# Projecting q, k and v by half groups, with attention heads between the row tiles, in a one-core hybrid decoder layer

## The chip, the core and the metric

The program runs on one core of a Trainium2 chip, as one launch. The metric is device time in microseconds (us) of that launch. TensorE is the matrix engine (PE in the profile, PEld its weight loads), VectorE is DVE, ScalarE is ACT, GpSimd is POOL, and SP only issues transfers. All arithmetic inputs are float32.

## The reference, cut to what matters

One layer of a decoder with two mixers on the same normalised input `hn`. The attention mixer has three groups of eight heads; group g has a window and a dilation of (128, 1), (512, 4) or (2048, 16). The prompt has 512 tokens, the decoding batch 8 tokens.

```python
u = hn @ w_in                                  # 520 rows x 1024, q, k, v among its columns
q = _rope(_rmsnorm(q.reshape(b, t, 24, 64), q_norm_w), pos)
k = _rope(_rmsnorm(k.reshape(b, t, 24, 64), k_norm_w), pos)
for g, (win, dil) in enumerate(((128, 1), (512, 4), (2048, 16))):
    o, lse = _dilated_attn_prompt(q[:, :, 8*g:8*g+8], k[...], v[...], win, dil)
    new_bufs.append(stack([kg, vg])[:, -min(win, 512):])
alpha = softmax(stack(lses))                   # groups merged per head slot
```

With 512 prompt tokens, group 0 is attention inside blocks of 128 tokens and to the block before. In groups 1 and 2 a query sees keys of its own residue class modulo 4 (group 2: modulo 16, by a mask). The other mixer is a chunked state-space scan (SSD) with 32 heads. The new key and value rows are outputs too.

## The kernel before

Every weight matrix is cut into items of 1 MB (`ITEMS`), which pass through two slots: SP loads `w_raw`, ACT rounds it to `wH` (float32r), and DVE takes the rest, `wL = w_raw - wH` (the plan's step `split`, L1178 and L1511). A projection adds three products, xH·wH, xL·wH and xH·wL, for each of the eight 128-row pieces of the contraction.

All engines walk one list of steps, `PLAN`, in its order; each engine does its own part of each step and waits on semaphores where it must. So a late step on an engine delays every later step of that engine. PSUM has eight banks. A bank is taken by TensorE (`take`) once whoever read its last content has freed it (`free`).

The attention part treats one group after the other.

- **Rows.** `("rm", g, s, half)` is half of the contraction for the 512 columns of q, k or v of a group. `proj_rows` (L578 to L596) works on five row tiles: four of 128 prompt tokens and one with the 8 decoding tokens. Tokens are the stationary operand and the 512 weight columns the moving one. Five banks, 0 to 4, stay open over the two halves. In groups 1 and 2 the stationary operand takes every fourth token (`slice(B + t, R, NT)`), so that a row tile is a residue class.
- **Norm and rotary, per row tile of q and k.** ACT squares the bank (L1204), DVE sums per head (L1526), ACT takes Ln and Exp (L1210, L1213), DVE multiplies (L1539, frees the bank) and forms the cosine part (L1543), POOL the sine part (L1080), and DVE adds them into `st` (L1552). v is copied by ACT to `vv` (L1191).
- **`turn`.** TensorE transposes `st` into banks 5 to 7, and ACT copies them to `qT` and `kT` (L1286). All four tiles of q are turned in one step, and so are those of k.
- **Heads.** Then come the eight heads: `scores` on TensorE (L678; L685 for the block before, in group 0 only), the scaled and masked copy and the maximum on DVE (L1655 to L1669), the exponentials on ACT (L1294, L1298), `probs`: transposes on TensorE (L694, L699) and copies to `PT` by ACT (and by DVE for the second bank, L1679), `values`: the product with v (L715, L718), copied by ACT to `oU` (L1320) for each pair of heads. ACT's exponentials are part of the step `scores`.
- **Filling.** `BESIDE_HEADS` puts pieces of one row tile (24 matmuls of 512 columns) between the heads of group 0, two between those of group 1, and 96 matmuls of 260 columns of the gate `za` between those of group 2.

After the third group there is a barrier, then the merge of the groups and the decoding tokens' attention, then the SSD part. There `ssdE` (L852 to L856) spreads a row of log decays over 128 partitions for each of a unit's two heads, with a contraction over 64 partitions (`id2`, `ac2`); it does so 16 times.

Of the kernel before, what the change touches and what calls it, by code (L numbers as in the profile page):

```python
# [19 lines left out]
F32 = mybir.dt.float32  # L20
F32R = mybir.dt.float32r
# [33 lines left out]
NKEYS = P  # L55

# [5 lines left out]
def weight_items():  # L62

    items = [("rm", g, s, half) for g in range(NG) for s in "qkv" for half in range(2)]
    items += [("za", 0), ("za", 1), ("dt", 0)]
    for g in range(GROUPS):
        items.append(("bc", g))
        for j in range(2 * g, 2 * g + 2):
            items += [("x", j), ("z", j)]
    items += [("gs", j) for j in range(4)]  # L70
    for j in range(2):
        items += [("ga", 2 * j), ("ga", 2 * j + 1), ("ba", j)]
    items += [("bs", j) for j in range(KD)]
    items += [("wo", j) for j in range(4)]
    return items
# [6 lines left out]
BESIDE_HEADS = {1: {0: 7}, 2: {0: 7, 1: 5}}  # L82
SPREAD_FIRST = 5
SLOTS_S = 5
PHASE_ENDS = (5, 10, 13)

SHAPES = {"rm": (4, 512), "dt": (KD, P), "bs": (UNITS, P), "ba": (4, 512)}


def item_units(i):  # L90

    return tuple(range({"rm": 0, "dt": 1, "bs": 1, "ba": 4}.get(ITEMS[i][0], 2)))


def plan():
# [18 lines left out]
    for g in range(NG):  # L114
        for s in "qkv":
            whole("rm", g, s, 0)
            if (g, s) == (0, "q"):
                out.append(("rope",))
            if s == "v":
                out.append(("turn", g, 0))  # L120
            whole("rm", g, s, 1)
        out.append(("turn", g, 1))


        if g + 1 < NG:
            out.append(("split", ITEM_AT["rm", g + 1, "q", 1]))
            beside = [("rowtile", g + 1, t, k) for t in BESIDE_HEADS[g + 1] for k in range(KD)]
        else:
            beside = []
            for unit in range(2):  # L130
                za_uses.append(proj("za", 0, unit=unit))
                _, i, units = out.pop()
                beside += [("proj", i, units, k) for k in range(KD)]
        total, steps = len(beside), 3 * SLOTS + 2
        count = 0
        for h in range(SLOTS + 2):
            for step in (("scores", g, h), ("probs", g, h - 1), ("values", g, h - 2)):
                if 0 <= step[2] < SLOTS:
                    out.append(step)
                    count += 1  # L140
                    while beside and total - len(beside) < total * (count + 2) / steps:
                        out.append(beside.pop(0))


# [18 lines left out]
    for i in range(n):  # L163
        out.append(("key", i))
        if i == 3:
            out.append(("exps",))
# [85 lines left out]


PLAN = plan()


# [62 lines left out]
def hybrid_kernel(nc, xT, wpack, params, consts, sel_in, state_conv, ssm_in, caches,  # L319
                  y_out, tail_out, ssmp_out, kvp_out, ssms_out, kvs_out):  # L320
    ctx = ExitStack()
    with ctx:
# [3 lines left out]
        def sb(name, shape, dt=F32):  # L326
# [28 lines left out]
        st = a1.tile("st", [P, 2, NT, T])  # L355
        qT = a1.tile("qT", [P, HP, T])
        kT = a1.tile("kT", [P, HP, T])
        vv = a1.tile("vv", [P, NT, T])
        ropeA = a1.tile("ropeA", [P, 2, RT, HD])
        ropeB = a1.tile("ropeB", [P, 2, RT, HD])  # L360
        pt_at = a1.at
        sq = a1.tile("sq", [P, 2, T])
        ss = a1.tile("ss", [P, 2, SLOTS])
        rst = a1.tile("rst", [P, 2, SLOTS])
        qn = a1.tile("qn", [P, T])
        t1 = a1.tile("t1", [P, T])
        t2 = a1.tile("t2", [P, T])
        Sx = a1.tile("Sx", [P, 2, 2 * NT - 1, P])

        PT = Arena(nc, pt_at, end).tile("PT", [P, 2, 2 * NT - 1, P])  # L370
# [70 lines left out]
        ac2 = a3.tile("ac2", [2 * HEADS, T], F32R)  # L441
        id2 = a3.tile("id2", [2 * HEADS, HEADS], F32R)
# [41 lines left out]
        names = """squares_added ac_parts_ready act_order b_rows_ready b_spread_ready b_spread_used bc_samples_kept cache_shifted cached_v_used  # L484
# [4 lines left out]
            gate_ready half_item_used head_pair_out head_scales_ready head_sums_ready  # L489
            k_stored keys_scored keys_turned last_state_ready log_decays_masked masked_cb_ready maxima_sums_ready  # L490
# [4 lines left out]
            sample_dt_ready sample_exponents sample_exps sample_probs sample_probs_turned  # L495
# [3 lines left out]
            states_before_ready tables_loaded v_rows_ready v_stored weight_high_ready  # L499
# [4 lines left out]
        names += [f"cache_loaded{i}" for i in range(RING)]  # L504
# [14 lines left out]
        def cm_bank(i, s, hf):  # L519
            if ITEMS[i] == ("za", 0):  # L520

                return banks[((2, 3), (5, 7))[s][hf]]
# [6 lines left out]
        def qk_count(g, si, t):  # L529
            return (g * 2 + si) * (NT + 1) + t  # L530
# [12 lines left out]
        def pv_done(eng, n):  # L543

            if n % 2:
                g, hp = n // SLOTS, n % SLOTS // 2
                banks[6].full(eng, ("O", g, hp))
# [3 lines left out]
        def row_bank(g, s, t):  # L551

            return banks[BESIDE_HEADS.get(g, {}).get(t, t) if s == "q" else t]

# [4 lines left out]
        merge_banks = [banks[i] for i in (2, 6, 0, 3, 7, 1)]  # L559
# [4 lines left out]
        def _(pe):  # L564
            nbar = [0]
            turn_c = [0]
# [7 lines left out]
            def row_columns(g, t):  # L574
                return slice(0, P) if t == NT else (slice(B + P * t, B + P * (t + 1)) if g == 0 else slice(B + t, R, NT))

            def proj_rows(i, g, s, half):
                for t in range(NT + 1):  # L578
                    if s == "q" and t in BESIDE_HEADS.get(g, {}):
                        continue  # L580
                    bk = row_bank(g, s, t)
                    if half == 0:
                        bk.take(pe, ("rm", g, s, t))
                    cols = row_columns(g, t)
                    for k in range(4):
                        kk = 4 * half + k
                        if t == 0 and (g, s) == (0, "q"):
                            pe.wait_ge(S["x_low_ready"], kk + 1)
                        for n, (a, b) in enumerate(((xH, wH), (xL, wH), (xH, wL))):
                            mm = pe.matmul(bk.tile[:, :], a[:, kk, cols], wslot(b, i)[:, k, :],  # L590
                                           start=(kk == 0 and n == 0), stop=(kk == KD - 1 and n == 2))
                    if half == 1:
                        mm.then_inc(bk.filled, 1)
                    elif t == NT:
                        mm.then_inc(S["half_item_used"], 1)
                ends[i] = (banks[NT].filled, banks[NT].uses["rm", g, s, NT]) if half else (S["half_item_used"], i // 2 + 1)  # L596
# [28 lines left out]
            for step in PLAN:  # L625
# [11 lines left out]
                elif op == "proj":  # L637
# [3 lines left out]
                    if it[0] == "rm":  # L641
                        proj_rows(i, *it[1:])
                    else:
                        proj_cols(i, a[1], a[2] if len(a) > 2 else None, *it)
                elif op == "rowtile":

                    g, t, kk = a
                    i = ITEM_AT["rm", g, "q", kk // 4]
                    pe.wait_ge(S["weight_low_ready"], i + 1)
                    bk = row_bank(g, "q", t)  # L650
                    if kk == 0:
                        bk.take(pe, ("rm", g, "q", t))
# [1391 lines left out]
```

## Time and profile before

| | |
|---|---|
| median of three runs | 1187.37 us (1184.84 to 1188.95) |
| the profiled execution | 1187.57 us |
| its span in the trace | 1185.8 us |
| TensorE busy | 1097.8 us (93%) |
| VectorE, ScalarE, GpSimd busy | 656.7, 499.4, 219.8 us |
| mean granted clock | 0.94 |

A view's time runs from the start of the span. Busy time of PE counts a matmul from its start to its modelled end, and neighbours overlap; the distance from start to start is what tells the rate. "clock" is the granted TensorE clock: 1.00 is 2.4 GHz, 0.50 is 1.2 GHz, and a stretch between has both. Matmuls of full float32 (scores, values) are recorded as two each. The rows themselves are given below in numbered groups.

### The profile page before, as it was taken

What the parts mean: (1) busy time and instruction counts of PE and PEld (TensorE: products, weight loads), DVE (VectorE), ACT (ScalarE), POOL (GpSimd) and SP (SyncE); (2) the same over time, 40 slices, a digit from 0 to 9 for tenths busy, and PEclk for the clock granted to TensorE, in tenths of its full rate; (3) what the DMA queues carried; (4) which work ended last, traced back from release to release, by engine and by line L of the source; (5) the groups of instructions that cost most, each with busy time, mean ns of one, the idle gap of its engine ahead of it and who ended that gap; (6) DMA issues with size and microseconds to landing.
All of it is one profiled execution on the core that took longest, in us unless ns stands there. A gap on an engine that the chain in (4) does not pass through costs nothing.

```text
span 1185.8 us, 19650 instructions
## 1 busy us (share of the span) xinstructions
PE 1097.8 (93%) x7838; PEld 1010.2 (85%) x7838; DVE 656.7 (55%) x936; ACT 499.4 (42%) x1130; POOL 219.8 (19%) x209
## 2 busy tenths in 40 slices
PE   4999989999999989895999999999998999689998
PEld 3887779977988779775999899898998999689998
DVE  6663527622462347237677677776764466834342
ACT  5334533345333544102554645656445566612210
POOL 0330003400231000000211220221120589500000
PEclk9998899989999899756999999999999999789999
DMA  8546102580242047145056246254446899432221
GB/s 348 213 169 276 55 1 116 213 329 1 107 168 81 1 151 246 58 152 232 1 219 235 109 162 254 110 218 163 182 175 273 343 360 343 155 144 80 100 98 46
DMA packets 29819, 198.14 MB, mean 167 GB/s; under 512 B 4104, under 2 KB 6280, under 8 KB 20224
## 3 DMA queue, kind: packets, MB, share of 16 engines
q1 hardware_dynamic: 25712, 183.35, 40.5%
q0 software_dynamic: 4016, 13.54, 3.0%
q8 instruction: 62, 1.02, 0.3%
q14 instruction: 29, 0.24, 0.1%
HBM read 180.16 MB, written 104.70 MB: 240 GB/s over the span
## 4 chain that ended last, share of the span: by engine, by line
PE 73%; DVE 11%; ACT 7%; issue 4%; DMA 2%; POOL 2%; SPq 0%; DVEq 0%; ACTq 0%; POOLq 0%
PE bank L618 36%; PE bank L590 16%; DVE cacc L1575 2%; PE bank L813 2%; PE bank L715 2%; ACT wH L1136 2%; PE bank L678 2%; PE bank L767 2%; POOL t L1080 2%; PE bank L884 1%; PE bank L654 1%; DVE wL L1511 1%; DMA slot<-in_state_ssm 1%; PE bank L902 1%; PE bank L876 1%
## 5 line engine op out<-in xcount | busy, mean ns | idle before, releaser
L1511 DVE TENSOR_TENSOR wL<-w_raw,wH 128x2048 fp32r<-128x2048 f32 (+1 forms) x63 | 145.0, 2302 | 155.0 <-ACT wH L1136 152.9
L618 PE MATMUL bank<-xH,wH 128*128 128x260 f32 x976 | 207.9, 294 | 8.1 <-DVEq L1455 6.9
L618 PE MATMUL bank<-xH,wL 128*128 128x260 f32 x976 | 198.1, 285 | 0.0
L618 PE MATMUL bank<-xL,wH 128*128 128x260 f32 x976 | 197.8, 284 | 0.0
L1136 ACT CAST wH<-w_raw 128x2048 fp32r<-128x2048 f32 (+1 forms) x63 | 119.2, 1892 | 136.2 <-PE bank L618 84.8
L618 PEld LDWEIGHTS bank<-xH,wH 128*128 128x128 f32 x976 | 152.0, 191 | 18.8 <-issue 16.6
L618 PEld LDWEIGHTS bank<-xH,wL 128*128 128x128 f32 x976 | 152.0, 190 | 0.0
L618 PEld LDWEIGHTS bank<-xL,wH 128*128 128x128 f32 x976 | 152.0, 190 | 0.0
L590 PE MATMUL bank<-wH,xH 128*128 128x512 f32 x336 | 136.7, 407 | 10.0 <-DVE xL L1490 6.0
L590 PE MATMUL bank<-wH,xL 128*128 128x512 f32 x336 | 134.6, 401 | 0.0
L590 PE MATMUL bank<-wL,xH 128*128 128x512 f32 x336 | 134.6, 401 | 0.0
L590 PEld LDWEIGHTS bank<-wH,xH 128*128 128x128 f32 x336 | 84.0, 250 | 21.2 <-issue 7.0
L1080 POOL TENSOR_TENSOR t<-qn,ropeB 128x256 f32<-128x256 f32 (+1 forms) x60 | 56.0, 951 | 246.4 <-DVE qn L1539 246.3
L590 PEld LDWEIGHTS bank<-wL,xH 128*128 128x128 f32 x336 | 84.1, 250 | 7.8
L590 PEld LDWEIGHTS bank<-wH,xL 128*128 128x128 f32 x336 | 84.3, 251 | 7.4
L1575 DVE SCALAR_TENSOR_TENSOR cacc<-buf,wcv,cacc 128x544 f32<-128x544 f32 x72 | 56.5, 784 | 17.3 <-ACT cacc L1251 15.1
L1294 ACT ACTIVATE Sx<-Sx,nm 128x128 f32<-128x128 f32 x96 | 37.6, 392 | 57.9 <-DVE nm L1669 57.8
L1381 ACT ACTIVATE Lb<-bank,nac 128x128 f32<-128x128 f32 x128 | 36.7, 369 | 47.1 <-PE bank L862 44.3
L1104 POOL TENSOR_TENSOR Eb<-Eb,CT 128x512 f32<-128x512 f32 x32 | 54.0, 1707 | 11.7 <-ACT Eb L1372 11.7
L618 PE MATMUL bank<-yH,wH 128*128 128x260 f32 x256 | 52.6, 287 | 3.5 <-DVE yL L1928 3.5
L618 PE MATMUL bank<-yL,wH 128*128 128x260 f32 x256 | 52.5, 287 | 0.0
L618 PE MATMUL bank<-yH,wL 128*128 128x260 f32 x256 | 52.2, 285 | 0.0
(285 smaller groups left out, 1916.9 us busy)
## 6 DMA issues: line engine op xcount, KB each, us to landing
w_raw<-in_weights SPq DMA_DIRECT2D x62, 1024.0 KB, 5.3
out_kvs<-in_cache SPq DMA_DIRECT2D x16, 2044.0 KB, 10.2
ring<-in_cache SPq DMA_DIRECT2D x48, 256.0 KB, 3.2
slot<-in_state_ssm SPq DMA_DIRECT2D x16, 512.0 KB, 5.9
out_ssm_s<-slot POOLq DMA_DIRECT2D x16, 512.0 KB, 6.0
out_kvs<-in_cache SPq DMA_DIRECT2D x8, 508.0 KB, 8.8
out_kvp<-st POOLq DMA_DIRECT2D x9, 256.0 KB, 2.3
out_kvp<-vv POOLq DMA_DIRECT2D x9, 256.0 KB, 4.6
```

Of the source, the lines that this page charges most:

```text
L590: mm = pe.matmul(bk.tile[:, :], a[:, kk, cols], wslot(b, i)[:, k, :], start=(kk == 0 and n == 0), stop=(kk == KD - 1 and n == 2))
L618: mm = pe.matmul(bk[hf].tile[:, 0:HALF], wslot(w, i)[:, k, s * P:(s + 1) * P], x[:, k, hf * HALF:(hf + 1) * HALF], start=(k == 0 and n == ...
L678: mm = pe.matmul(bk.tile[:, t * P:(t + 1) * P], qT[o:o + HD, hp, t * P:(t + 1) * P], kT[o:o + HD, hp, t * P:(t + 1) * P], start=True, stop ...
L715: mm = pe.matmul(out, vv[:, t, h * HD:(h + 1) * HD], PT[:, n % 2, t, :], start=(t == 0), stop=True, skip_group_check=True)
L767: mm = pe.matmul(banks[6].tile[:, c:c + B + 1:B], KT[:, n % 2, hp, :], qd[:, q0, :], start=True, stop=True, skip_group_check=True)
L1080: ins = nc.gpsimd.tensor_tensor(o[:, :, x, :], v[:, :, 1 - x, :], rb, ALU.mult)
L1104: nc.gpsimd.tensor_tensor(Eb[:, u % 2, e, :], Eb[:, u % 2, e, :], CT[:, 0:T], ALU.mult).then_inc(S["scaled_c_ready"], 1)
L1136: return nc.scalar.copy(out, in_)
L1294: ins = A(Sx[:, n % 2, t, :], Sx[:, n % 2, t, :], ACT.Exp, bias=nm[:, n % 2, t:t + 1], accum_out=lst[:, g, t, h:h + 1])
L1381: ins = A(Lb[:, e, c, :], banks[5 + e].tile[:, c * P:(c + 1) * P], ACT.Exp, bias=nac[:, c, n:n + 1])
L1511: TT(wL[:, i % 2, 0:k * n], raw[:, i % 2, 0:k * n], wH[:, i % 2, 0:k * n].bitcast(F32), ALU.subtract)\
L1575: ins = STT(out=cacc[:, :], in0=bb[:, w:w + CONV], scalar=wcv[:, cu, w:w + 1], in1=cacc[:, :], op0=ALU.mult, op1=ALU.add)
```

## The change

The unit of work in the attention part becomes a half group `x` (0 to 5), four heads. An item is now all 1024 contraction rows of 256 columns of q, k or v, so there are still 18 such items.

- **Rows.** A row tile of q or k is one step of 24 matmuls with 256 moving columns, in natural token order for all groups. Three banks (0, 1, 2) go round in a ring (`row_ring`) instead of five.
- **v by columns.** The weights are stationary and the tokens move, 260 at a time: 24 matmuls in a slot, two slots for each unit of 128 columns. A unit takes two ring banks; ACT copies them to `vT` (three copies), TensorE transposes `vT` (four transposes and one for the decoding tokens) into a ring bank and bank 6, and DVE copies these to `vv` and `qS`.
- **Residue classes.** For groups 1 and 2 the classes are formed by a strided destination in ACT's copies to `qT`, `kT` and `vT`.
- **Order.** `PLAN` runs over 84 slots (five for q, five for k, four for v of each half group). In slot j: row tile j, exponentials of a head, `roped` of tile j-2, `norm` of j-1, square and sum of j (`copy`), `turn` of j-3, the copies of v, and then a head's scores, probs or values. A head takes four successive slots: scores, exponentials, probs, values. The heads of half group x run beside the row tiles of x+1; those of the last half group beside `za`, in eight slots more.
- **Banks.** All turns, the second probs bank of group 0 and the decoding values share bank 6; scores have bank 3 (and 4), probs bank 5, values bank 7. `qn`, `t1`, `t2` are double, of half width. Stored rows leave in 48 transfers by POOL instead of 24, with half as long rows.
- **SSD.** `ac2` and `id2` get a second copy on partitions 64 to 127, made once by ACT (`dtrows`); the two matmuls of `ssdE` use one half each, and both banks are taken ahead of the first.
- The banks of `za` and of the merge are renamed; step `exps` of the merge becomes `mergeexps`.

```diff
-    items = [("rm", g, s, half) for g in range(NG) for s in "qkv" for half in range(2)]
+    items = [(s, x) for x in range(HALVES) for s in "qkv"]
...
-BESIDE_HEADS = {1: {0: 7}, 2: {0: 7, 1: 5}}
+SLOT_ROWS = 2 * (NT + 1) + 4
...
+    def side_steps():
+        at = {}
+        for n in range(NG * SLOTS):
+            x, m = divmod(n, HH)
+            first, gap = (SLOT_ROWS * (x + 1) + 4 * m, 1) if x < HALVES - 2 else (SLOT_ROWS * (x + 1) + 3 * m, 1)
+            if x == HALVES - 1:
+                first = SLOT_ROWS * HALVES - 2 + 2 * m
+            for d, op in enumerate(("scores", "exps", "probs", "values")):
+                at.setdefault(first + d * gap, []).append((op, n))
+        return at
...
+    def slot(j):
+        mine = at.get(j, [])
+        out.extend(x for x in mine if x[0] == "exps")
+        step("roped", 2)
+        step("norm", 1)
+        step("copy", 0)
+        step("turn", 3)
+        for ago, op in ((0, "vcopy"), (1, "vturn"), (1, "vrows")):
+            if 0 <= j - ago < len(rows) and ITEMS[rows[j - ago][0]][0] == "v" and rows[j - ago][1] % 2:
+                out.append((op, rows[j - ago][0], rows[j - ago][1] // 2))
+        out.extend(x for x in mine if x[0] != "exps")
...
+def row_ring():
+    out, c = {}, 0
+    for step in PLAN:
+        if step[0] == "rows":
+            out["row", step[1], step[2]] = c % 3
+            c += 1
+        elif step[0] == "vcols" and step[3] == 0:
+            for hf in range(2):
+                out["col", step[1], step[2], hf] = (c + hf) % 3
+            c += 2
+        elif step[0] == "vturn":
+            out["vturn", step[1], step[2]] = c % 3
+            c += 1
+    return out
...
+                    for kk in range(KD):
+                        for n, (x, w) in enumerate(((xH, wH), (xL, wH), (xH, wL))):
+                            mm = pe.matmul(bk.tile[:, 0:HC], x[:, kk, row_columns(t)], wslot(w, i)[:, kk, :],
+                                           start=(kk == 0 and n == 0), stop=(kk == KD - 1 and n == 2))
...
+                elif op == "vcopy":
+                    b0, b1 = (col_bank(i, unit, hf) for hf in range(2))
+                        by_class = vT[:, unit, 0:T].rearrange("p (r j) -> p j r", r=NT)
+                        cp(by_class[:, 0:first // NT, :], b0.tile[:, B:HALF].rearrange("p (j r) -> p j r", r=NT))
+                    free(b0)
+                    free(b1)
...
-                        pe.matmul(bk.tile[:, :], id2[:, 2 * u + e:2 * u + e + 1].to_broadcast([2 * HEADS, P]), ac2[:, :],
+                        o = 2 * HEADS * e
+                        pe.matmul(bk.tile[:, :], id2[o:o + 2 * HEADS, 2 * u + e:2 * u + e + 1].to_broadcast([2 * HEADS, P]), ac2[o:o + 2 * HEADS, :],
```

## Rows read from the trace of the kernel before

**Rows 1.** The page, part 2: TensorE busy and granted clock in 40 slices.
```profile
PE   4999989999999989895999999999998999689998
PEclk9998899989999899756999999999999999789999
```

**Rows 2.** Windows: each head stretch and the SSD stretch (stretch, us, busy by engine, clock).
```profile
106.43:167.14 60.71, 52.41 (x322) 44.74 (x320) 29.80 (x65) 33.01 (x129) 0.52 (x1) 0.83 0.16 64
250.01:296.93 46.92, 42.75 (x225) 34.35 (x224) 14.54 (x25) 25.24 (x81) 0.52 (x1) 0.89 0.21 83
378.49:426.50 48.01, 40.73 (x273) 35.15 (x272) 14.53 (x25) 26.28 (x82) 0.52 (x1) 0.89 0.01 2
562.40:913.00 350.60, 345.55 (x2849) 317.62 (x2848) 240.51 (x378) 190.69 (x426) 63.53 (x73) 1.00 0.44 171
```

**Rows 3.** The chain that ended last, whole span: start, us, what.
```profile
18.95 71.80 PE bank L590 x300
90.74 1.88 PE bank L668 x16
92.62 13.98 PE bank L590 x60
571.18 5.76 PE bank L618 x48
```

**Rows 4.** The chain in 140 to 170 us: one head of group 0.
```profile
152.59 0.22 PE bank L718 x2
153.83 1.10 PE bank L678 x8
155.06 0.70 DVE Sx L1655
158.31 0.54 ACT Sx L1294 x3
159.97 1.16 ACT Sx L1298 x6
161.13 0.48 ACT PT L1136
161.79 0.63 PE bank L694 x4
```

**Rows 5.** Groups of instructions by line, whole span: busy us, mean ns.
```profile
L1511 DVE TENSOR_TENSOR wL<-w_raw,wH 128x2048 fp32r<-128x2048 f32 x62 | 143.8, 2320 | 154.7 <-ACT wH L1136 152.6 <-DVE zs L1608 1.7 <-DVE zg L1566 0.2
L1136 ACT CAST wH<-w_raw 128x2048 fp32r<-128x2048 f32 x62 | 118.1, 1905 | 135.9 <-PE bank L618 84.8 <-PE bank L590 43.9 <-DMA w_raw<-in_weights 4.6
L1080 POOL TENSOR_TENSOR t<-qn,ropeB 128x256 f32<-128x256 f32 x48 | 45.1, 960 | 241.9 <-DVE qn L1539 241.9
L1204 ACT ACTIVATE sq<-bank 128x512 f32<-128x512 f32 x24 | 14.3, 599 | 34.2 <-PE bank L590 34.2
```

**Rows 6.** The same view, ScalarE only, 19 to 430 us.
```profile
L1210 ACT ACTIVATE ss<-ss,epsc 128x8 f32<-128x8 f32 x24 | 7.2, 298 | 12.5 <-DVE ss L1526 12.5
```

**Rows 7.** The tile oU: shortest, median, longest copy; group 0 contiguous, others strided.
```profile
L1136 ACT COPY oU<-bank x12: 587/1076/1109, 138.1 to 425.3; 128x512 f32<-128x512 f32 x12
```

**Rows 8.** Timeline of VectorE at the start.
```profile
24.51 1.92 DVE L1490 TENSOR_TENSOR xL<-xw,xH 128x520 fp32r<-128x520 f32 x3
27.12 2.29 DVE L1511 TENSOR_TENSOR wL<-w_raw,wH 128x2048 fp32r<-128x2048 f32 x1 [0.69 <-ACT wH L1136]
32.77 0.46 DVE L1500 SCALAR_TENSOR_TENSOR ropeB<-con,par 128x288 f32<-128x288 f32 x1
```

**Rows 9.** Windows around one gap of TensorE and the clock behind it.
```profile
158.00:162.80 4.80, 2.21 (x13) 1.65 (x12) 1.03 (x5) 4.20 (x17) 0.00 (x0) 1.00 0.00 0
162.80:166.20 3.40, 3.40 (x21) 3.40 (x22) 0.56 (x1) 0.26 (x1) 0.00 (x0) 0.50 0.00 0
```

**Rows 10.** Timeline of TensorE in one SSD unit.
```profile
602.22 1.09 PE L884 MATMUL bank<-Lb,xdt 128*64 128x128 f32 x16
603.24 0.72 PE L855 MATMUL bank<-ac,id 64*128 64x512 f32 x2
```

More of the change, by code:

```diff
@@ L112, in whole @@
         out.append(proj(*item))
[L114 to L142, printed above, removed]
@@ new lines, in plan, with step @@
+    rows = []
+    for i in range(3 * HALVES):
+        rows += [(i, t) for t in (range(4) if ITEMS[i][0] == "v" else range(NT + 1))]
+    za_steps = []
+    def slot(j):
+        def step(op, ago):
+            if 0 <= j - ago < len(rows):
+                i, t = rows[j - ago]
+                if ITEMS[i][0] != "v" and (op != "turn" or t < NT):
+                    out.append((op, i, t))
+        mine = at.get(j, [])
[8 more added lines that the diff above has]
+        out.extend(x for x in mine if x[0] != "exps")
@@ new lines, in plan @@
+    for j, (i, t) in enumerate(rows):
+        if t == 0 and ("split", i + 1) not in out:
+            out.append(("split", i + 1))
+        out.append(("vcols", i, t // 2, t % 2) if ITEMS[i][0] == "v" else ("rows", i, t))
+        if j == 0:
+            out.append(("rope",))
+        slot(j)
+    j = len(rows)
+    for unit in range(2):
+        za_uses.append(proj("za", 0, unit=unit))
+        _, i, units = out.pop()
+        za_steps += [("proj", i, units, k) for k in range(KD)]
+    late = max(at) + 1 - j
@@ L145, in tiles @@
+    for d in range(late):
+        out += za_steps[len(za_steps) * d // late:len(za_steps) * (d + 1) // late]
+        slot(j + d)
     def tiles(item, unit):
@@ L527, in wslot, with qk_count, kept_tiles, k_stores @@
             return w[:, i % 2, 0:k * n].rearrange("p (k n) -> p k n", k=k)
-        def qk_count(g, si, t):
-            return (g * 2 + si) * (NT + 1) + t
+        def qk_count(i, t):
+            return (2 * (i // 3) + i % 3) * (NT + 1) + t
+        def kept_tiles(x):
+            return (NT - 1,) if x < 2 else range(NT)
+        def k_stores(t, x):
+            return 16 * sum(t in kept_tiles(y) for y in range(x + 1))
+        def v_stores(x):
+            return 16 * sum(len(kept_tiles(y)) + 1 for y in range(x % 2, x + 1, 2))
         CV = {}
@@ L545, in pv_done, with row_bank, col_bank, turn_bank @@
             if n % 2:
-                g, hp = n // SLOTS, n % SLOTS // 2
-                banks[6].full(eng, ("O", g, hp))
+                banks[7].full(eng, ("O", n // 2))
             else:
                 eng.wait_ge(S["even_head_summed"], n // 2 + 1)
-        def row_bank(g, s, t):
-            return banks[BESIDE_HEADS.get(g, {}).get(t, t) if s == "q" else t]
+        def row_bank(i, t):
+            return banks[ROW_RING["row", i, t]]
+        def col_bank(i, unit, hf):
+            return banks[ROW_RING["col", i, unit, hf]]
+        def turn_bank(i, unit):
+            return banks[ROW_RING["vturn", i, unit]]
+        def score_bank(n):
+            return banks[3 if n < SLOTS else 3 + n % 2]
         def spread_bank(i):
             return banks[((7, 5) if i < 2 else (7, 6) if i < SPREAD_FIRST else (4, 6))[i % 2]]
-        merge_banks = [banks[i] for i in (2, 6, 0, 3, 7, 1)]
+        merge_banks = [banks[i] for i in (7, 0, 1, 2, 6, 3)]
         block = ctx.enter_context(nc.Block())
@@ L572, in barrier, with row_columns @@
                     pe.wait_ge(S["phase_ended"], 5 * nbar[0])
[L574 to L596, printed above, removed]
+            def row_columns(t):
+                return slice(0, P) if t == NT else slice(B + P * t, B + P * (t + 1))
             def proj_cols(i, units, tile, kind, j):
```

528 lines of the change are left out of this document (290 added, 238 removed).

## The prediction

> **What bounds the kernel now.** I read the page's slices first: TensorE is busy nearly everywhere, but between slices 3 and 15 its clock falls several times [rows 1]. Then the chain, for the true rate. TensorE runs 60 matmuls of 512 columns in 13.98 us, 233 ns each, and 48 of 260 columns in 5.76 us, 120 ns each; 16 transposes take 1.88 us [rows 3]. So a matmul costs what its columns cost (0.45 ns each), and a wide one isn't cheaper by column. Then the windows: the attention part is TensorE work from 18.95 us [rows 3] to 426.50 us [rows 2], 407.5 us, and the three head stretches in it run at a mean clock of 0.83, 0.89 and 0.89 [rows 2].
>
> How much of the 407.5 us is work? Row tiles: 1080 matmuls x 0.233 = 251.6. Turns: 96 transposes x 0.117 = 11.3. A head of group 0 has 7 score and 7 value matmuls, two records each at 0.11 [rows 4], and 7 transposes: 3.9 us, with some 0.1 at each of four changes of kind 4.3. A head of the others has 4 of each, 2.6. That is 8 x 4.3 + 16 x 2.6 = 76. The `za` pieces: 96 x 0.120 plus changes, 13.9. Sum 352.8. So about 55 us are lost now, nearly all in and just ahead of the heads: 17 us in group 0's 60.7, and about 10 in each of the other two, after taking out heads, pieces and turns.
>
> **The change part by part.**
>
> Work. q and k: 60 row tiles x 24 matmuls x 0.1185 (256 columns, by the rate above) = 170.6. v: 24 slots x 24 x 0.120 = 69.1. Turns 11.3 as before. v's transposes are new: 12 x 5 x 0.117 = 7.0. Heads 76, `za` 13.9. Sum 347.9, that is 4.9 less; the gain is v's, which had five row tiles and now has no tile for the eight decoding tokens. Everything else depends on what the new order loses.
>
> Start. The first row tile now needs all eight pieces of x at once. The last arrives at 24.51 + 1.92 = 26.4 us, and DVE is then in wL and the rotary tables until 33.2 [rows 8]. Before, five banks let TensorE go on meanwhile. Now the fourth row tile needs the first bank back: sum, Ln and Exp, multiply, about 1.6 us after 33.2. It starts at 34.9, with 8.5 us of work done since 18.95. Loss 7.4.
>
> Group 0's heads among row tiles (half groups 0 and 1, beside the rows of 1 and 2). Take the slot of a head's scores as j, its start as 0. Row tile 2.85, turn 0.25, scores 1.0, and 0.8 for the block before: TensorE leaves at 4.85. DVE starts when the first score bank is full, at 4.4, and needs 3.25 us to the exponentials (155.06 to 158.31); these take until 161.2, 2.9 us [rows 4]. So ACT is held until 4.4 + 3.25 + 2.9 = 10.6. Only then come, in ACT's order, Ln and Exp of row tile j (0.3 [rows 6] plus 0.2), the next square (0.6 at 512 columns [rows 5], 0.4 here) and the turn's copy. Waiting behind it are DVE's `norm` of j, which frees that row tile's bank at 11.5, and bank 6, free at 12.0. TensorE, meanwhile, has finished slot j+1 at 7.95. Four cases, by where the head falls in the 14 slots:
> - head 1: slot j+2 needs bank 6 twice (turn, then the second probs bank, each emptied before the other). It ends at 14.45 where its work would end at 12.0. Loss 2.5.
> - head 0: v's transpose has used up a ring bank, so the third row tile shares the first's bank, and waits for `norm` of the scores slot. DVE has had wL (2.3 us [rows 5]) and v's rows ahead of the scores. Loss 4.7.
> - head 2: v's first unit takes two ring banks at once, the second being that of tile j, free at 11.5; then wH (1.9 us [rows 5]) stands ahead of the turn's copy. Loss 3.9.
> - head 3: its exponentials stand ahead of `vcopy` (1.1 us), and the next row tile needs a bank that `vcopy` frees. Loss 4.0.
> With 0.3 between v's units this is 15.4 for each of two half groups, and 1.3 twice more where the last head's probs wait for bank 6 behind DVE's copy of v: 33.4.
>
> Groups 1 and 2. DVE takes 1.8 and ACT 1.6 for a head. The same four places lose 2.5, 0, 1.5 and 2.4, and 1.3 between v's units, because the strided copies cost more: a strided copy of 512 columns takes 1.08 against 0.59 [rows 7], so a turn's copy about 0.6 and `vcopy` about 1.5. That is 7.7 in each of two half groups, 6.7 in the last, where heads are three slots apart. The first half group, without heads, loses 2.9 at v's two changes. The tail (four heads beside `za`, DVE and ACT needing 3.7 us where TensorE has 4.5 us of other work) loses 1. A copy that writes 512 bytes apart isn't in the trace; from below it costs as a contiguous one, from above twice the strided one, together -7 to +12 us; I take the strided row.
>
> The sum of losses: 7.4 + 2.9 + 33.4 + 15.4 + 6.7 + 1 = 66.8.
>
> Clock. Now, a stretch of 4.8 us in which TensorE is busy 2.2 is followed by 3.4 us at 0.50, that is at 1.2 GHz [rows 9]. Each such stretch costs at least 1.7 us of work. The new order has six gaps of 3.6 to 4.7 us (heads 0, 2 and 3, twice). Bounds 0 and 12; I take 7.
>
> SSD. The two matmuls of `ssdE` take 0.72 us [rows 10]. The nearest row for small matmuls on different parts of the array is L884, 16 in 1.09 us [rows 10], where records of that size otherwise stand 0.11 apart [rows 4] and would take 1.8: its pairs, into the two column halves, run together. If row halves do so too, a pair saves about 0.3; sixteen pairs, in a stretch where TensorE is busy 345.6 of 350.6 us [rows 2]: -4. Bounds 0 and -5. The Trainium skill, TensorE: Matmul & The Clock Gate, Part 3 (row/col tiling), says that matmuls on distinct row groups run concurrently; by it the -5 holds, and no row here shows it for rows.
>
> At nothing: ACT's one copy of `ac2` (512 columns, some 0.6 us like the square of that width [rows 5]) stands in front of a wait for TensorE's last product of `dtrows`, which comes later than it. POOL's sine pair falls from 2 x 0.96 [rows 5] to some 1.1 in slots of over 3 us; even with five transfers to issue for v it is done before `roped` two slots later. Were that cover gone, about 1 us per v item, 6 in all. The weights' transfers are asked for two items ahead, some 28 us. Doubling the stored transfers costs only POOL's time. The renamed banks move no wait by more than a few tenths.
>
> Sum against the profiled execution, 1187.6 (the median shown is 0.2 lower): work -4.9, losses 66.8 - 54.7 = +12.1, clock +7, SSD -4: +10. I predict **1198 us**.
>
> **The rivals.**
> 1. Interleaving pays. The 33.4 and 15.4 + 6.7 us of ACT's lag are worked out head by head; if the engines catch up better, for instance because DVE gets to the scores sooner, and half of this (28) and the clock's 7 go away, the time is 1163; with all of it gone 1135. For it: ACT and DVE are idle half of every head stretch [rows 2], and heads no longer wait for a whole group's rows and turns. Against it: one head's exponentials block ACT for 2.9 us, and there are three ring banks where there were five. It decides once the losses with the clock fall by 10 us, i.e. below 64. The Trainium skill, Trace Analysis, Optimization Strategy, says that interleaving stretches with different busiest engines may improve performance; by it this rival holds. The same section reads regular gaps as a sign of too little SBUF or PSUM for the next tile, which is my own forecast's mechanism.
> 2. Gains and losses cancel: 1184 to 1191.
> 3. A copy or a bank is worse than I take it: strided writes at twice the strided row, bank 6 shared by turns, probs and v at more places, or clock stretches over 12 us. 1215 to 1230.
> 4. 256-column matmuls are held by their weight loads, and cost more than 118 ns: at 190 ns (the recorded load) q and k would take 103 us more, near 1300. The 260-column row at 120 ns, with a load each, speaks against it.
>
> **How the numbers follow.** 0.48 for my forecast (1191 to 1214), 0.33 for rival 1 (1140 to 1183), 0.10 for rival 2, 0.07 for rival 3, 0.02 for rival 4. What a measurement here can tell from no change is about 0.3%, 3.6 us. Rival 2 and the edges of its neighbours give 0.10 for the same; rival 1 and a little of rival 2 give 0.34 for faster; the rest, 0.56, is slower. The range, 8 in 10, takes in the strided copy's bound, a full clock loss, and half of ACT's lag gone: 1160 to 1214. The forecast's own range is 1191 to 1214.
>
> **What would show it.** In the changed trace the row matmuls should stand 118 to 120 ns apart; TensorE should wait, in the half groups beside group 0's heads, for DVE's `norm` multiply and for ACT (turn copies, `vcopy`), 15 us in each; the PE clock should show half-speed stretches behind these; the attention part should end near 440 us; the `ssdE` pair should start within some 10 ns. I am wrong if the attention part ends before 426 us: then ACT and DVE kept up, and the waits for them are under a microsecond a head. I am also wrong if the row tiles' pitch, or the stretch after the barrier, moves by more than a few us.

## The result, and the profile after

The changed kernel takes 1244.41 us (median of four runs, 1241.26 to 1246.80); the kernel before took 1187.30 us beside it. The ratio is 1.048, 95% interval 1.046 to 1.051. Slower was right, the size was not: 57 us where I had 10, and outside the range.

The profiled execution took 1241.26 us, 53.7 more than the one of before. The page of the changed kernel, parts 1 and 2, against [rows 1]:

```profile
PE 1124.1 (91%) x8834; PEld 1065.1 (86%) x8834; DVE 689.7 (56%) x1082; ACT 527.2 (43%) x1266; POOL 236.4 (19%) x293
...
PE   4979788899999889989599999999999898789998
...
PEclk9989999999999965555699999999999899889999
```

Read the line PEclk first. Its 15th to 20th digits are 6, 5, 5, 5, 5, 6: six slices at about half clock, where before there were three (7, 5, 6). TensorE is hardly idle there: the busy digits above them are 8 and 9, but for a 5 above the last. What is lower early on is its busy time (7 and 8 in the 5th to 8th digit), where heads now stand among the rows.

Windows over the four parts of the span (attention, decoding, the projection of `dt`, SSD and the rest) show what each contributes: stretch, us, busy time of PE, PEld, DVE, ACT and POOL, clock, DMA share, GB/s. After:

```profile
18.95:433.02 414.07, 368.55 (x2868) 347.12 (x2869) 230.16 (x415) 192.03 (x565) 88.11 (x168) 0.98 0.34 132
433.02:592.28 159.26, 142.93 (x1011) 134.19 (x1011) 55.31 (x83) 26.57 (x43) 0.00 (x0) 0.54 0.34 116
592.28:617.49 25.21, 16.34 (x94) 15.91 (x95) 19.04 (x33) 6.21 (x13) 0.00 (x0) 0.64 0.66 255
617.49:1239.50 622.01, 594.25 (x4859) 566.68 (x4858) 375.03 (x537) 290.79 (x630) 148.07 (x121) 0.97 0.47 180
```

The first three parts in the kernel before:

```profile
18.95:426.50 407.55, 383.76 (x1872) 335.34 (x1873) 198.25 (x271) 164.11 (x429) 69.52 (x84) 0.95 0.34 133
426.50:537.57 111.07, 99.32 (x1011) 90.76 (x1011) 55.22 (x83) 26.47 (x43) 0.00 (x0) 0.77 0.50 166
537.57:562.40 24.83, 16.66 (x94) 16.23 (x94) 18.68 (x31) 5.60 (x12) 0.00 (x0) 0.64 0.64 259
```

The attention part is 6.5 us longer, the SSD part 1.4 shorter, the projection of `dt` 0.4 longer. Two changes partly cancel in the attention part: TensorE's idle time grew from 23.8 to 45.5 us, and its time at half clock fell from 44.4 to 13.7 us. The decoding part (merge of the groups, cached keys and values) is 48.2 us longer: the same 1011 matmuls, with VectorE and ScalarE equally busy, at a clock of 0.54 in place of 0.77. Nothing in this part was changed but names of banks.

What happens at its start? TensorE, in the timeline of the changed kernel:

```profile
441.96 0.60 PE L811 MATMUL bank<-con,lst 128*8 128x128 f32 x4
442.40 0.60 PE L829 MATMUL bank<-con,ring 128*128 128x128 f32 x4
448.61 0.77 PE L668 MATMUL bank<-xH,wH 128*128 128x260 f32 x2 [5.61 <-DVEq L1547]
449.18 0.64 PE L668 MATMUL bank<-xL,wH 128*128 128x260 f32 x2
```

The same piece of `za` in the kernel before:

```profile
437.36 0.48 PE L618 MATMUL bank<-xH,wH 128*128 128x260 f32 x2 [0.86 <-DVEq L1455]
```

VectorE, in the timeline of the changed kernel:

```profile
442.15 0.68 DVE L1800 COPY mT<-bank 8x512 f32<-8x512 f32 x1 [0.24 <-DVE qd L1792]
442.97 0.68 DVE L1800 COPY lT<-bank 8x512 f32<-8x512 f32 x1
...
447.36 1.04 DVE L1800 COPY lT<-bank 8x512 f32<-8x512 f32 x1
```

TensorE transposes the six merge tiles into six banks, and DVE copies them out in the order maxima, sums, group by group (L1800). Behind the first cached key's transposes (L829) stands the first piece of `za`'s second unit, which takes banks 2 and 3. In the kernel before these two held the tiles copied first and second. The diff rewrites the list `merge_banks`, from (2, 6, 0, 3, 7, 1) to (7, 0, 1, 2, 6, 3). The first three entries hold the maxima of the groups and the last three the sums, so the copies, which go by turns, took the banks as 2, 3, 6, 7, 0, 1 before, and take them as 7, 2, 0, 6, 1, 3 now: bank 3 is the last of six. The piece waits 5.61 us, until that copy ends at 448.4. Before, the same wait was 0.86 us. The clock's records in the trace show half from 445.5 us, 2.5 us into the wait, for 150.2 us without a break. Behind the wait TensorE is busy all the time by the profile (89.39 of 89.40 us) and still at half:

```profile
448.60:538.00 89.40, 89.39 (x417) 89.40 (x418) 24.50 (x27) 19.61 (x30) 0.00 (x0) 0.50 0.34 119
```

The last cached key ends at 540 us. Before, the keys ran at full clock, and this part had 54.6 us at half, from 487.1 on, behind the last key. So some 95 us at half are new, and they lie in the wait and the keys.

### The profile page after: what moved, and what is told of

The parts are those of the page before. It is cut to its first block, busy times and chain, and to the rows that moved or that the text cites. A ratio compares the mean times of both kernels' runs of the same rounds, so it can differ in the third digit from the quotient of the medians.

```text
span 1239.5 us, 22367 instructions
## 1 busy us (share of the span) xinstructions
PE 1124.1 (91%) x8834; PEld 1065.1 (86%) x8834; DVE 689.7 (56%) x1082; ACT 527.2 (43%) x1266; POOL 236.4 (19%) x293
## 4 chain that ended last, share of the span: by engine, by line
PE 71%; DVE 13%; ACT 8%; issue 4%; DMA 3%; SPq 0%; DVEq 0%; POOL 0%; ACTq 0%; POOLq 0%
PE bank L668 35%; PE bank L702 10%; PE bank L717 5%; PE bank L842 3%; DVE cacc L1624 2%; PE bank L888 2%; ACT Sx L1385 2%; PE bank L753 2%; PE bank L829 2%; ACT wH L1220 2%; PE bank L790 1%; PE bank L962 1%; PE bank L980 1%; PE bank L954 1%; DVE yL L2026 1%
## 5 line engine op out<-in xcount | busy, mean ns | idle before, releaser
L668 PE MATMUL bank<-xH,wH 128*128 128x260 f32 x976 | 214.0, 302 | 15.2 <-DVEq L1547 12.4
L668 PEld LDWEIGHTS bank<-xH,wH 128*128 128x128 f32 x976 | 157.7, 198 | 23.6 <-issue 21.0
L702 PE MATMUL bank<-wH,xH 128*128 128x256 f32 x480 | 144.8, 302 | 28.2 <-ACTq L1223 11.5
L668 PEld LDWEIGHTS bank<-xL,wH 128*128 128x128 f32 x976 | 157.7, 197 | 0.0
L702 PE MATMUL bank<-wL,xH 128*128 128x256 f32 x480 | 138.6, 289 | 0.0
L702 PE MATMUL bank<-wH,xL 128*128 128x256 f32 x480 | 138.3, 288 | 0.0
L702 PEld LDWEIGHTS bank<-wH,xH 128*128 128x128 f32 x480 | 93.9, 196 | 35.6 <-issue 31.0
L1161 POOL TENSOR_TENSOR t<-qn,ropeB 128x128 f32<-128x128 f32 (+1 forms) x120 | 61.4, 531 | 173.1 <-DVE qn L1726 172.9
L702 PEld LDWEIGHTS bank<-wH,xL 128*128 128x128 f32 x480 | 94.3, 197 | 0.0
L702 PEld LDWEIGHTS bank<-wL,xH 128*128 128x128 f32 x480 | 94.3, 197 | 0.0
L717 PE MATMUL bank<-xH,wH 128*128 128x260 f32 x192 | 43.3, 299 | 12.7 <-DVEq L1547 8.5
```

The costliest lines, as they stand in the source:

```text
L668: mm = pe.matmul(bk[hf].tile[:, 0:HALF], wslot(w, i)[:, k, s * P:(s + 1) * P], x[:, k, hf * HALF:(hf + 1) * HALF], start=(k == 0 and n == ...
L702: mm = pe.matmul(bk.tile[:, 0:HC], x[:, kk, row_columns(t)], wslot(w, i)[:, kk, :], start=(kk == 0 and n == 0), stop=(kk == KD - 1 and n = ...
L717: mm = pe.matmul(bk[hf].tile[:, 0:HALF], wslot(w, i)[:, k, unit * P:(unit + 1) * P], x[:, k, hf * HALF:(hf + 1) * HALF], start=(k == n == ...
L1161: ins = nc.gpsimd.tensor_tensor(o[:, :, y, :], v[:, :, 1 - y, :], rb, ALU.mult)
```

## The experiments

Ten kernels, each timed against the kernel before on the same chip. "Changed" means the kernel after the diff. The label behind each heading is the name that the recorded expectations use.

**1. Other banks for the waiting piece** (`e1_za_banks`).
```diff
+            if (ITEMS[i], s) == (("za", 1), 1):
+                return banks[(2, 7)[hf]]
```


> The changed kernel, with the second unit of the gate item za 1 put into banks 2 and 7, whose merge transposes VectorE copies first and second, instead of 2 and 3, of which 3 is copied last. Theory A (one bank wait of 5.9 us behind the barrier tips the granted clock to half speed for 150 us): the wait falls to about 1 us as before, the clock stays at 1.00 until the merge's spreads, and the time comes to 1187 + 6.5 (attention part) - 1 (SSD part) = 1193 us, 1188 to 1198. Rival B (the clock there is low for another reason, for instance the leaner attention part ahead of it, and the wait only happens to precede it): only the wait itself goes, 5 us, 1239 us.

Measured: 1239.35 us, ratio 1.044 (1.041 to 1.046), the value of rival B. My theory seemed to fall. The timeline says why it had not been tested:

```profile
448.69 0.60 PE L831 MATMUL bank<-con,ring 128*128 128x128 f32 x4
450.10 0.48 PE L670 MATMUL bank<-xH,wH 128*128 128x260 f32 x2 [0.81 <-DVEq L1549]
...
450.89 0.60 PE L831 MATMUL bank<-con,ring 128*128 128x128 f32 x4
452.49 1.02 PE L844 MATMUL bank<-qd,KT 128*128 128x2 f32 x8 [1.00 <-issue]
```

The long wait is gone, two short ones are left. The first was there in the kernel before as well. The second is for bank 6, which the sample scores (L844) take: the rename had also put it fourth in the order of the copies, where it was third. The clock still fell, from 454.6 us for 143.4 us.

**2. The kernel before with the clash alone** (`e2_before_bank_clash`).
```diff
-        merge_banks = [banks[i] for i in (2, 6, 0, 3, 7, 1)]
+        merge_banks = [banks[i] for i in (2, 6, 0, 7, 1, 3)]
```


> The kernel before, with nothing changed but the order of the merge's banks, so that bank 3 is the last of six to be copied. Theory A: TensorE waits some 5 us longer ahead of the first piece of za 1, the clock falls there and stays at half speed until the decoding part ends, and the kernel before becomes as slow as the changed one: 1187 + 5 + 42 = 1234 us. Rival B: +5 us, 1192 us.

Measured: 1232.54 us, ratio 1.038 (1.036 to 1.040), as theory A had it. The wait is 5.6 us here (433.3 to 438.9 us), and the clock falls in it, at 435.9. In the window from there to the end of the part TensorE is at half clock throughout:

```profile
436.00:582.56 146.56, 132.95 (x922) 125.11 (x923) 47.68 (x70) 21.77 (x34) 0.00 (x0) 0.50 0.33 108
```

So three numbers in a list cost the old kernel 45 us, with none of the new order in it. The wait itself, 5.6 us in place of 0.9, is 5 us of that; the rest is clock.

**3. The changed kernel with neither wait** (`e5_no_bank_wait`). Experiment 1, and the list so that banks 7 and 2 are copied first and second and bank 6 third:
```diff
-        merge_banks = [banks[i] for i in (7, 0, 1, 2, 6, 3)]
+        merge_banks = [banks[i] for i in (7, 6, 1, 2, 0, 3)]
```


> The changed kernel with the za(1, 1) products in banks 2 and 7, and the merge transposes renamed so that banks 7 and 2 are copied out first and second and bank 6 third, as in the kernel before. In the first run with other banks two waits stayed, 1.1 us at the first key's transposes and 1.3 us where the sample scores take bank 6, and the clock still fell. Theory A (any wait of over a microsecond of TensorE in this stretch of small matmuls, and only that, puts the clock at half for some 150 us and costs 40 to 48 us): both waits under 0.3 us, the clock stays full until the spreads' stretch, and the kernel takes 1190 to 1198 us. Rival B (the stretch is slow because of what comes ahead of it, the new order of the attention part, whatever the banks): the clock still falls near 450 us, and the time stays at 1236 to 1242 us.

Measured: 1195.27 us, ratio 1.006 (1.003 to 1.010). Windows over the attention part and the decoding part:

```profile
18.95:439.02 420.07, 374.53 (x2868) 353.14 (x2868) 229.56 (x415) 191.97 (x564) 88.07 (x168) 0.96 0.34 130
439.02:550.11 111.09, 99.16 (x1011) 90.76 (x1011) 55.24 (x83) 26.28 (x43) 0.00 (x0) 0.78 0.50 166
```

The decoding part is back at 111.09 us, where before it was 111.07. TensorE's timeline has the first short wait still, and none at L844, where experiment 1 had 1.00 us:

```profile
449.83 0.47 PE L670 MATMUL bank<-xH,wH 128*128 128x260 f32 x2 [0.81 <-DVEq L1549]
...
451.05 1.02 PE L844 MATMUL bank<-qd,KT 128*128 128x2 f32 x8
```

With experiment 1 this isolates the second wait: 44 us between two kernels of which one has a wait of 1.0 us more (46 us when each is taken against the kernel before beside it).

**4. The small wait in the kernel before** (`e6_before_small_wait`).
```diff
-        merge_banks = [banks[i] for i in (2, 6, 0, 3, 7, 1)]
+        merge_banks = [banks[i] for i in (2, 7, 0, 3, 6, 1)]
```


> The kernel before with one name moved: bank 6, which the sample scores take, holds the fourth merge transpose copied out in place of the third; the projection's banks stay copied first and second. This asks how large a wait must be. Theory A (a wait of 1 to 1.5 us in this stretch already tips the clock): 1225 to 1235 us, with the clock at half from about 440 us. Rival A2 (only a wait of several us tips it, as the 5.9 us one did, and the small ones of the changed kernel are harmless): 1187 to 1190 us, with one wait of 1.2 us more and the clock as in the kernel before.

Measured: 1228.03 us, ratio 1.034 (1.029 to 1.038), as theory A had it. TensorE's timeline:

```profile
437.20 0.48 PE L618 MATMUL bank<-xH,wH 128*128 128x260 f32 x2 [0.86 <-DVEq L1455]
...
439.56 1.02 PE L767 MATMUL bank<-qd,KT 128*128 128x2 f32 x8 [0.95 <-issue]
```

VectorE in that timeline, the fourth copy:

```profile
438.35 1.05 DVE L1699 COPY lT<-bank 8x512 f32<-8x512 f32 x1
```

The view names "issue" as the releaser of the second wait, but it ends 0.16 us behind the fourth copy, and appears only when bank 6 is the fourth: it is the bank. The first wait, of 0.86 us, is in the kernel before too, and by itself left the clock alone. A second of 0.95 us, 2.4 us later, was followed by 139.9 us at half. No run here says where between one such wait and two the line is.

**5. Useless work in place of the wait** (`e10_filled_wait`). The changed kernel, its banks as the diff has them, with 48 matmuls that nobody reads ahead of the first key's transposes:
```diff
+                        if n == 0:
+                            for r in range(48):
+                                pe.matmul(bk.tile[:, 0:HALF], wslot(wH, 0)[:, r % KD, 0:P], xH[:, r % KD, 0:HALF],
+                                          start=True, stop=True, skip_group_check=True)
```


> The changed kernel with its banks as they are, and 48 matmuls of 260 columns added whose result is overwritten and never read, ahead of the first key's transposes: 5.8 us of useless work that fills the 5.6 us wait for bank 3. Theory A (the idle time itself, not the bank order nor DVE's lateness, puts the clock at half for 150 us): although work is added, the kernel gets faster by 40 to 48 us, 1196 to 1204 us; the 1.3 us wait for bank 6 behind it may still tip the clock, and then it stays at 1238 to 1244 us and the dose is below 1.3 us. Rival B (the clock falls for the key stretch's own small matmuls behind any late DVE): 1240 to 1248 us.

Measured: 1201.95 us, ratio 1.011 (1.008 to 1.015) to the kernel before, which is 42 us under the changed kernel, although it does 5.9 us more work, and in theory A's range. The timeline shows neither wait left (the added matmuls are L830, of which the view shows the last 21):

```profile
449.80 2.72 PE L830 MATMUL bank<-xH,wH 128*128 128x260 f32 x21
452.36 0.60 PE L833 MATMUL bank<-con,ring 128*128 128x128 f32 x4
452.88 0.48 PE L668 MATMUL bank<-xH,wH 128*128 128x260 f32 x2
```

On its page the clock is low for three digits in this part (the 18th to 20th), as in the kernel before:

```profile
PEclk9999998999999999956799999999999999889999
```

This separates the idle time of TensorE from everything else that a late bank could do. DVE's copies come as late behind TensorE's transposes as in the changed kernel, the banks are the same, and only the idle time is filled. It doesn't tell idle time from a lack of wide matmuls: what fills it is 260 columns wide.

**6. The exponentials later in ACT's order** (`e4_exps_late`). Experiment 1, with a head's `exps` at the end of the slot, behind the row tile's steps and v's:
```diff
-        out.extend(x for x in mine if x[0] == "exps")
         step("roped", 2)
...
             out.append((op, rows[j - ago][0], rows[j - ago][1] // 2))
+        out.extend(x for x in mine if x[0] == "exps")
```


> The kernel of e1_za_banks, with a head's exponentials moved from the beginning of ScalarE's work in a slot to behind the norm, the square, the turn's copy and vcopy of that slot. Theory C (in the slots after a head's scores ScalarE's order makes row tiles wait, 15 us in each of the two half groups of group 0, about 6 in the others): the waits of 4.8, 3.5 and 4.0 us in front of row and column tiles go, and the time falls by 15 to 30 us against e1_za_banks, to some 1168. Rival D (what is lost there is a head's own latency of scores, maximum, exponentials, transposes, whatever the order): within 5 us of e1_za_banks.

Measured: 1229.94 us, ratio 1.036 (1.033 to 1.038): 9.4 under experiment 1, less than the 15 to 30 that I expected, and more than rival D's 5. The waits of TensorE in the attention part of the changed kernel (what waited, for what: us in total, times, the longest):

```profile
PE bank L702 <- ACTq L1223: 11.5, 5, 3.7
PE bank L702 <- DVEq L1547: 9.8, 5, 4.5
PE bank L717 <- DVEq L1547: 8.5, 4, 3.1
PE bank L702 <- DVE xL L1582: 6.9, 6, 5.6
PE bank L717 <- ACTq L1223: 4.1, 4, 1.5
```

And of this one:

```profile
PE bank L775 <- DVEq L1549: 8.6, 2, 4.3
...
PE bank L704 <- ACTq L1225: 6.0, 5, 1.3
PE bank L775 <- ACTq L1225: 5.1, 4, 2.1
...
PE bank L704 <- DVEq L1549: 3.3, 4, 1.4
```

(L702 and L717 there are L704 and L719 here.) The waits of rows and of v's columns for their banks have shrunk or gone; in their place the second bank of a head's probabilities (L775) waits until DVE has copied v's transposes out of bank 6, 4.3 us at the longest.

**7. and 8. The order with the banks put right** (`e7_no_bank_wait_exps_late`, `e8_no_bank_wait_exps_mid`). Experiment 3 with `exps` last in the slot, as in 6, and with `exps` between `turn` and v's steps, whose edit is:
```diff
-        out.extend(x for x in mine if x[0] == "exps")
         step("roped", 2)
...
         step("turn", 3)
+        out.extend(x for x in mine if x[0] == "exps")
```

> The banks of e5_no_bank_wait and, in each slot, a head's exponentials behind the row tile's norm, copy, turn and v's steps on ACT, as in e4_exps_late, which was worth 9.4 us by itself. Theory A: both gains add, 1178 to 1188 us, the attention part ending near 429 us and the clock full until the spreads. Rival B: 1228 to 1232 us, as e4_exps_late.

> As e7_no_bank_wait_exps_late, but the exponentials stand behind norm, copy and turn and ahead of v's copy, transposes and row steps. In e4_exps_late the waits of 4.6 us at a head's probs came back behind v's copy. If v's copy is what made the probs late (theory), heads 2 and 3 wait less at the probs and more at v's banks: 3 us either way of e7, 1176 to 1190 us. If ACT's total lag sets the loss wherever it is put (rival), the time is within 2 us of e5_no_bank_wait less 9.

Measured: 1189.13 us, ratio 1.000 (0.998 to 1.002), and 1182.06 us, ratio 0.995 (0.992 to 0.997). The first is a us above the range I expected (1178 to 1188), the second inside its own (1176 to 1190), though I had the two within 3 us of each other. The middle place is 7 us better than the last, and 13 better than the diff's. Its windows, attention and decoding part:

```profile
18.95:419.13 400.18, 364.90 (x2868) 342.62 (x2869) 229.53 (x416) 193.65 (x565) 87.56 (x168) 1.00 0.36 136
419.13:530.24 111.11, 99.58 (x1010) 90.91 (x1011) 55.27 (x83) 26.44 (x43) 0.00 (x0) 0.77 0.51 165
```

In the attention part TensorE is idle for 35.3 us, where experiment 3 had 45.5, and its clock is at half for a single 3.4 us, where it was for 30.7. The place of the exponentials saves waits. That the saved waits save so much clock is less sure: the changed kernel, with the waits of experiment 3, had 13.7 us at half, and the two profiled executions lie 6 us further apart than the medians.

**9. The state-space rows alone** (`e3_ssd_rows_alone`). The kernel before with the doubled `ac2` and `id2` of the diff and nothing else.
```diff
...
-                        pe.matmul(bk.tile[:, :], id2[:, 2 * u + e:2 * u + e + 1].to_broadcast([2 * HEADS, P]), ac2[:, :],
+                        o = 2 * HEADS * e
+                        pe.matmul(bk.tile[:, :], id2[o:o + 2 * HEADS, 2 * u + e:2 * u + e + 1].to_broadcast([2 * HEADS, P]), ac2[o:o + 2 * HEADS, :],
```

> The kernel before, with the doubled ac2 and id2 alone, so that the two matmuls of ssdE work on different halves of the array's rows. In the changed kernel's trace a unit of the SSD part is shorter by 0.22 us. Theory: 16 units, -3.5 us, 1184 us. Rival (ScalarE's exponentials are next in line at once, or the copy of ac2 costs as much): within 1 us of 1187.

Measured: 1184.54 us, ratio 0.998 (0.996 to 0.999), 2.8 us less. The pair in one unit of the changed kernel, beside [rows 10]:

```profile
643.17 0.50 PE L933 MATMUL bank<-ac,id 64*128 64x512 f32 x2
```

**10. Pieces in the later waits** (`e9_pieces_in_waits`). Experiment 8, with seven of `bc`'s eight pieces held back from beside the keys and put ahead of `samplemax` (3), `sampleprobs` (1) and `ownvalues` (3).
```diff
-        use = next(piece)
+        if i <= n - KD:
+            use = next(piece)
...
         if i == 2:
+            for _ in range(3):
+                next(piece)
             out.append(("samplemax",))
...
+    next(piece)
+    out.append(("sampleprobs",))
+    for _ in range(3):
+        next(piece)
+    out.append(("ownvalues",))
```

> e8_no_bank_wait_exps_mid with seven of the eight bc product pieces (6 matmuls each, 0.8 us) held back from beside the keys: three go ahead of samplemax, one ahead of sampleprobs and three ahead of ownvalues, where TensorE waits 2.76, 1.53 and 2.38 us and behind which its clock is at half for 54.6 us. Theory A (waits of this size between small matmuls tip the clock): the waits shrink to a fraction of a us, 5 us of waiting is filled, and the clock stays full until the wait before dt: about 15 us of half-clock loss on top of 5, so 1160 to 1170 us. Rival B (the value products, 2 columns each, pull the clock down themselves): only the filled waits are gained, 1175 to 1180 us, and half clock still begins near 480 us.

Measured: 1179.95 us, ratio 0.992 (0.990 to 0.995), which can't be told from experiment 8. Rival B for the time; its half clock begins 8 us earlier than the 480 that rival B had. Windows over its decoding part:

```profile
466.00:472.00 6.00, 6.00 (x58) 6.00 (x57) 0.74 (x1) 2.69 (x5) 0.00 (x0) 1.00 0.72 213
472.00:479.00 7.00, 7.00 (x29) 6.13 (x29) 2.42 (x4) 0.24 (x1) 0.00 (x0) 0.53 0.29 80
479.00:492.00 13.00, 11.21 (x75) 9.26 (x73) 5.63 (x14) 0.67 (x2) 0.00 (x0) 0.63 0.00 1
492.00:520.00 28.00, 28.00 (x419) 23.58 (x420) 6.89 (x10) 0.00 (x0) 0.00 (x0) 0.56 0.52 161
```

Here the clock falls at 472.4 us, and by the profile TensorE was busy in every instant of the six us before it (the ends of matmuls are modelled, so this is no proof of full work). What stood there from 464.4 on were the last keys without a piece beside them: four transposes and eight matmuls of 2 columns each in turn. In experiment 8 the same keys, with the pieces beside them, ran at full clock up to 479 us. The clock came back twice for 3.4 us, from 479.2 and from 492.8, in or just behind pieces, and fell for the last time at 496.2 us among the value products, narrow work too, with no wait of over 0.5 us since 485. So the waits weren't what held the clock down in that stretch. The kernel before says the same: there the half clock begins at 487.1 us, and the 2.3 us wait of that stretch only at 487.6. By these traces both the waits and the narrow matmuls bear on the clock, and the pieces of 260 columns work against them.

## Why the prediction was wrong

**The step that failed** is the last sentence of the costs at nothing: "The renamed banks move no wait by more than a few tenths". I had not followed the list against the order in which DVE empties the banks. That step moved one wait from 0.86 to 5.61 us, and behind it lay another, of 1.0 us for bank 6, which shows once the first is short (experiment 1). The decoding part, which the forecast left as it was, became 48.2 us longer. By experiments 3 and 5 undoing or filling the waits takes the changed kernel from 1244 to 1195 and 1202 us. No rival had this; rival 3's "a bank is worse than I take it" looked at the attention part, and its 1215 to 1230 is still short. Without the renames my number would have stood, 1195.27 against 1198, but by luck in part: the losses in the attention part were some 13 us smaller than my sum has them and the work 6 us more, as shown below.

**Clock, 7 us.** For the attention part the sum came out, the changed kernel has 13.7 us at half there, which can cost 6.8; but it was in three stretches and not behind each of six gaps, and experiment 3, with the same waits, had 30.7 us. The mistake was its reach. I bounded the loss by one 3.4 us stretch for each gap, from [rows 9], and kept to the part where the row tiles are. The merge and the keys are built of small matmuls, and there the clock fell in or just behind a wait and stayed at half for 140 to 150 us, in five kernels (the changed one and experiments 1, 2, 4 and 6). The Trainium skill, TensorE: Matmul & The Clock Gate, Part 1, says that the gate follows how busy TensorE has recently been. The trace agrees for the fall behind a wait, and disagrees with busy time as the whole measure: in the windows above TensorE is busy 133 of 146.6 us at 0.50 (experiment 2), and 89.39 of 89.40 at 0.50 (the changed kernel).

**Attention: work -4.9, losses +12.1.** Predicted end near 440 us; found 433.02 in the changed kernel and 439.02 in experiment 3, which runs the same steps. TensorE's idle time in the part is the same in both, 45.5 us; they differ in how many short half-clock stretches they drew (13.7 and 30.7 us). The losses without the clock come to about 54 us, where my sum has 66.8. The parts, each gap from start to start less a matmul's pitch:
- Row matmuls of 256 columns stand 119 ns apart, as predicted (118.5). But the first of a tile takes 0.20 to 0.22 us, so 24 take 2.93 to 2.96 us and not 2.84. I had such a cost at the changes of kind in a head, and not here. Over 60 tiles it is about 6 us more work, so the work was level rather than 4.9 less. They are not held by their weight loads: rival 4 is out.
- Start: the fourth row tile begins at 35.03 us (predicted 34.9), a loss of 7.5 us (predicted 7.4).
- Heads of group 0 beside rows. In the timeline of the changed kernel, a row tile waits behind the first head, and v's second bank behind the third:

```profile
84.56 0.55 PE L702 MATMUL bank<-wH,xH 128*128 128x256 f32 x1 [4.48 <-DVEq L1547]
...
126.24 0.39 PE L717 MATMUL bank<-xH,wH 128*128 128x260 f32 x1 [3.12 <-DVEq L1547]
```
  These gaps are 4.6 and 3.4 us (predicted 4.7 and 3.9). The first comes only once: at its place in the second half group TensorE loses 2.0. Head 3's are 3.5 and 3.9 (predicted 4.0), and head 1's are 2.1 and 2.4, each in two pieces (predicted 2.5). In all group 0's heads lose 27.8 us (predicted 33.4).
- v's changes in the first half group: 1.5 and 1.2 (predicted 2.9 together). Groups 1 and 2: 1.4, 1.0, 1.9 and 1.4 in a half group, 5.6 together (predicted 7.7). The last half group: 3.4 (predicted 6.7), and its heads beside `za` 1.5 (predicted 1).

The cause I gave, ACT held by one head's exponentials, is what experiment 8 undoes: the same steps with another order on ACT are 13 us faster than experiment 3. With that order the kernel is 6 us faster than the one before (4 to 9), and about 3 of these are the state-space rows'. What is left for the interleaving, some 3.5 us, is hardly clear of the noise. Rival 1 had it end near 1163; no run reached that.

**State-space rows, -4.** Measured 2.8 less (interval 0.8 to 4.9) alone, and 1.4 less between the two traces' last parts. The pair takes 0.50 us where it took 0.72, and its two matmuls start 3 to 4 ns apart, where it was 333 to 340. The mechanism was right, the saving is 0.22 a unit and not 0.3.

No other of the costs at nothing shows in the time: the `dt` part moved by 0.4 us, and the SSD part by no more than its rows give.

**What stays open.** Why the same engine regains its clock within a few us among wide matmuls, and not through some 90 us of keys, is not settled. Experiment 10 points at the narrow matmuls. But the keys with their pieces hold full clock in experiment 3, and half clock in experiment 1, with the same matmuls. From a few us behind the first key on they kept one level in every kernel here, and I have no run that says why.

## What to carry to other kernels

When a diff renames PSUM banks, list for each bank who empties it, in that engine's order, and set it against who takes it next; a name is a wait. Price a wait by what stands behind it: among wide matmuls it cost its own length and a little clock (in the changed kernel 13.7 us at half for 45.5 us of idle time), ahead of this stretch of small ones a second wait of 1.0 us cost 44 us. If such a wait can't be moved, try to fill it, even with work that nobody reads: here that gave back 42 us.

## What the runs showed of the hardware

- A half clock of 140 to 150 us with TensorE busy over 90% of it by the profile, begun just behind two waits of about 1 us (experiments 1, 4 and 6), or in one of over 5 (the changed kernel and experiment 2); adding 5.9 us of useless matmuls made the kernel 42 us faster.
- Within the same key loop the pieces of 260 columns take 133 ns a matmul at full clock (6 in 0.80 us, experiment 5), and 240 at half (6 in 1.44 us, the changed kernel).
- The clock also fell (472.4 us in experiment 10) with no wait in the 40 us ahead of it, in a run of 2-column matmuls and transposes.
- Two matmuls of 512 columns on the two row halves of the array start 3 to 4 ns apart, and take 0.50 us together.
